# Block-diagonal fp32 products of a decoder trunk cut into 64x64 and 32x32 tiles of the TensorE array

## The reference

```
# A (RWKV-7), 4 heads of 64
kk = kk / max(sqrt(sum(kk*kk over the head)), 1e-12)
mean, var = mean and variance of y over the head;  bonus = sum(r*k*r_k over the head) * v
# B (HGRN2) and C (retention), 4 heads of 64
o * rsqrt(mean(o*o over the head) + EPS)
# C: rotary embedding of q and k, 4 heads of 32 channels each
t1, t2 = split(t, 2);  concat(t1*cos - t2*sin, t1*sin + t2*cos)
# D (RG-LRU), 4 blocks of 64
r = sigmoid(einsum('btgi,gij->btgj', yb, w_a) + b_a);  i = sigmoid(einsum('btgi,gij->btgj', yb, w_x) + b_x)
```

## Time and profile before

| | |
|---|---|
| median of 3 runs | 1134.91 us |
| lowest and highest | 1130.58 and 1135.85 us |
| profiled execution, its own time | 1135.37 us |
| its span (first to last instruction) | 1133.2 us |
| mean granted TensorE clock | 0.976 |
| PE busy | 1086.7 us (96%) |
| DVE, ACT, POOL busy | 586.3, 333.9, 372.9 us |

### The profile page before, as it was taken

One profiled execution on the slowest core, in us unless ns is written; L12 is line 12 of the kernel. 1 busy time (PEld: TensorE's weight loads), 2 busy tenths in 40 slices (PEclk: granted clock), 3 DMA queues, 4 the chain that ended last, 5 costly groups with the idle time before them and its releaser, 6 DMA issues.

```text
span 1133.2 us, 23369 instructions
## 1 busy us (share of the span) xinstructions
PE 1086.7 (96%) x10052; PEld 849.1 (75%) x10052; DVE 586.3 (52%) x1045; ACT 333.9 (29%) x533; POOL 372.9 (33%) x343
## 2 busy tenths in 40 slices
PE   5999999889899999999999999999999989999997
PEld 5876787667677777777777787777777768887885
DVE  3368943885445323333433316747777586423544
ACT  4285212421422222122121133236545341011321
POOL 2231543311316522122212233335433347663000
PEclk8889999989989999999999999999999999999998
DMA  9600111200101011011011021111111116412221
GB/s 356 241 1 19 47 48 55 65 28 24 34 25 38 27 34 39 26 34 39 25 34 35 21 73 37 38 52 40 35 38 35 39 53 249 139 38 93 75 93 56
DMA packets 80134, 70.29 MB, mean 62 GB/s; under 512 B 4128, under 2 KB 68896, under 8 KB 80032
## 3 DMA queue, kind: packets, MB, share of 16 engines
q1 hardware_dynamic: 74560, 49.34, 14.0%
q10 hardware_dynamic: 5472, 19.47, 4.7%
HBM read 64.60 MB, written 4.19 MB: 61 GB/s over the span
## 4 chain that ended last, share of the span: by engine, by line
PE 89%; DVE 7%; ACT 2%; issue 1%; DMA 1%; SPq 0%; ACTq 0%; DVEq 0%
PE bank L581 51%; PE bank L627 8%; PE bank L1082 8%; PE bank L678 4%; PE bank L1043 1%; DVE slots L2060 1%; PE bank L784 1%; DVE slots L1651 1%; PE bank L899 1%; PE bank L903 1%; PE bank L654 1%; PE bank L685 1%; PE bank L815 1%; PE bank L845 1%; PE bank L645 1%
## 5 line engine op out<-in xcount | busy, mean ns | idle before, releaser
L581 PE MATMUL bank<-hn_hi,w_hi 128*128 128x512 f32 x880 | 365.1, 415 | 4.5 <-ACT slots L1194 2.8
L581 PE MATMUL bank<-hn_lo,w_hi 128*128 128x512 f32 x880 | 344.7, 392 | 0.0
L581 PE MATMUL bank<-hn_hi,w_lo 128*128 128x512 f32 x880 | 344.1, 391 | 0.0
L496 POOL CAST w_hi<-w_raw 128x512 fp32r<-128x512 f32 x110 | 86.4, 786 | 573.7 <-PE bank L581 572.4
L581 PEld LDWEIGHTS bank<-hn_hi,w_hi 128*128 128x128 f32 x880 | 165.8, 188 | 46.9 <-issue 4.6
L581 PEld LDWEIGHTS bank<-hn_hi,w_lo 128*128 128x128 f32 x880 | 165.9, 188 | 36.2
L581 PEld LDWEIGHTS bank<-hn_lo,w_hi 128*128 128x128 f32 x880 | 166.3, 189 | 31.4 <-issue 1.9
L498 POOL TENSOR_TENSOR w_lo<-w_raw,w_hi 128x512 fp32r<-128x512 f32 x110 | 155.2, 1411 | 8.8
L1216 ACT ACTIVATE stage<-bank 128x512 f32<-128x512 f32 x64 | 38.3, 598 | 222.7 <-PE bank L581 195.6
L1803 DVE TENSOR_TENSOR stage<-stage,bank 128x512 f32<-128x512 f32 x48 | 33.0, 688 | 64.6 <-PE bank L627 63.5
L1194 ACT ACTIVATE slots<-bank 128x512 f32<-128x512 f32 x42 | 25.1, 598 | 119.7 <-PE bank L581 118.5
(11 more groups left out here) (322 smaller groups left out, 1630.4 us busy)
## 6 DMA issues: line engine op xcount, KB each, us to landing
w_raw<-in_w_in SPq DMA_DIRECT2D x110, 256.0 KB, 2.8
slots<-in_w_mod SPq DMA_DIRECT2D x16, 512.0 KB, 11.2
slots<-in_x SPq DMA_DIRECT2D x8, 512.0 KB, 9.4
w_branch<-in_w_branch SPq DMA_DIRECT2D x32, 128.0 KB, 2.7
slots<-in_w_mod ACTq DMA_DIRECT2D x8, 512.0 KB, 4.8
slots<-in_w_out ACTq DMA_DIRECT2D x8, 512.0 KB, 5.7
xr<-in_x ACTq DMA_DIRECT2D x8, 512.0 KB, 3.6
out<-xr ACTq DMA_DIRECT2D x8, 512.0 KB, 2.6
```

The source lines that it names most:

```text
L496: nc.gpsimd.tensor_copy(w_hi[p][:, :, :], w_raw[p][:, :, :]).then_inc(s_w_hi_ready, 1)
L581: last = mm(o, w[p][:, k4, :], h[:, k, n * HALF:(n + 1) * HALF], start=(p == 0 and k4 == 0 and q == 0), stop=(p == 1 and k4 == 3 and q == 2))
```

## The change

Each of the block-diagonal products is replaced by products of its nonzero blocks, each on its own tile on the diagonal of the array. `over_heads` issues two 64 x 64 products (rows and columns 0 to 63, then 64 to 127), D's gates do the same with `lru_w`, and the rotation issues four 32 x 32 products. All write the same bank as before, each its own partitions, over the same 512 tokens. The semaphore is counted on the last of the two or four. Nothing else is changed, and no product changes its place in the order: 36 products become 80 (8 to 16 gates, 4 to 16 for the rotation, 24 to 48 head sums), which adds 88 matmul records and 88 weight loads.

```
@@ D's gates
-                        mm(bank[q][:, :], lru_w[:, 2 * g + j, :], slot(4 + j)[:, n * HALF:(n + 1) * HALF],
-                           start=True, stop=True).then_inc(s_gates_done, 1)
+                        for r in (slice(0, 64), slice(64, 128)):
+                            last = mm(bank[q][r, :], lru_w[r, 2 * g + j, r], slot(4 + j)[r, n * HALF:(n + 1) * HALF],
+                                      start=True, stop=True)
+                        last.then_inc(s_gates_done, 1)
@@ new, and head_sums
+            def over_heads(o, src):
+
+                for r in (slice(0, 64), slice(64, 128)):
+                    last = mm(o[r, :], blockones[r, r], src[r, :], start=True, stop=True)
+                return last
+
...
-                        mm(bank[4 + 2 * j + n][:, :], blockones,
-                           slot(src + j)[:, n * HALF:(n + 1) * HALF], start=True, stop=True).then_inc(s_head_sums, 1)
+                        over_heads(bank[4 + 2 * j + n], slot(src + j)[:, n * HALF:(n + 1) * HALF]).then_inc(s_head_sums, 1)
@@ the rotation
-                    mm(bank[4 + 2 * q + n][:, :], tb("perm"), slot(20 + q)[:, n * HALF:(n + 1) * HALF],
-                       start=True, stop=True).then_inc(s_rot_done, 1)
+                    for r0 in range(0, P, 32):
+                        r = slice(r0, r0 + 32)
+                        last = mm(bank[4 + 2 * q + n][r, :], tb("perm")[r, r], slot(20 + q)[r, n * HALF:(n + 1) * HALF],
+                                  start=True, stop=True, tile_position=(r0, r0))
+                    last.then_inc(s_rot_done, 1)
@@ A's mean (the bonus at L990 and B's sums at L1069 in the same way)
-                    mm(bank[4 + 2 * j + n][:, :], blockones, slot(4 + j)[:, n * HALF:(n + 1) * HALF],
-                       start=True, stop=True).then_inc(s_a_mean_done, 1)
+                    over_heads(bank[4 + 2 * j + n], slot(4 + j)[:, n * HALF:(n + 1) * HALF]).then_inc(s_a_mean_done, 1)
```

More of the change, by code:

```diff
@@ L989, in _ @@
                     pe.wait_ge(s_roots, 8 + 2 * j + n + 1)
-                    mm(bank[4 + 2 * j + n][:, :], blockones, slot(8 + j)[:, n * HALF:(n + 1) * HALF],
-                       start=True, stop=True).then_inc(s_a_bonus_done, 1)
+                    over_heads(bank[4 + 2 * j + n], slot(8 + j)[:, n * HALF:(n + 1) * HALF]).then_inc(s_a_bonus_done, 1)
             turn_tile(BI)
@@ L1068, in _ @@
                     pe.wait_ge(s_squares, 6 + 2 * n + j + 1)
-                    mm(bank[4 + 2 * j + n][:, :], blockones, slot(12 + j)[:, n * HALF:(n + 1) * HALF],
-                       start=True, stop=True).then_inc(s_head_sums, 1)
+                    over_heads(bank[4 + 2 * j + n], slot(12 + j)[:, n * HALF:(n + 1) * HALF]).then_inc(s_head_sums, 1)
             fill(73)
```

## The result

The changed kernel took **1137.04 us** (median of 20 runs, 1133.69 to 1139.38) against 1134.46 for the kernel before (20 runs, 1130.58 to 1138.03): a ratio of **1.0026**, 95% interval 1.0016 to 1.0037, which is +1.8 to +4.2 us. The forecast was 1136.7 us and +1.8. The profiled execution's span is 1134.9 us, where 1135.0 was forecast.

The account below looks back on a forecast made before the run. TensorE, busy 96% of the span, was taken as the bound. The terms 0 + 0 + 0.15 + 1.48 + 0.15 = 1.78, say +1.8 us, on a median of 1134.91 gave 1136.7 us, range 1131.5 to 1141.5.

Parts of the forecast that it names:

- The streaming term: At every cut product, the blocks run side by side and stream in 0.86 us as before; 0 us added.
- Rival 1: At every burst, tiles writing one bank do not run side by side; head-sum bursts take 6.86 us; 1164 us, chance 0.05.
- rival 4: At the bursts, small tiles are quicker, half the rows or columns halving the record; -10.3 us, 1124.6 us, chance 0.02.
- The switch term: Going between whole-array and tiled products costs TensorE 0.37 us a burst, 0.15 in and 0.22 out; eight bursts.
- The cover: At each burst, switch time ahead of a wait is hidden; D's gates and the rotation were put at 0 us.
- The gates: D's gates: way in hidden by DVE's convolution, way out by PE's wait for ACT; 0 us, bounds -0.05 to 0.37.
- The rotation: DVE takes its first result over 3 us after PE finishes, PE then waits 4.37 us; 0 us, at most 0.37.
- Turn 0: Starts out of a wait, nothing to drain; way out 0.2 less 0.05 for shorter load: 0.15 us, bounds 0 to 0.5.
- Branch B's sums: Way in, 0.15 us, passes down the chain of ACT and DVE; way out vanishes in PE's wait; 0.15 us.
- The waits: PE's waits at L581 for ACT and at L784 and L627 for DVE get shorter by about 0.2 us each.
- Rival 2: The granted clock falls at tiled bursts; one fall 1140.1 us, chance 0.12; two or three 1143 to 1147 us, chance 0.04.
- Rival 3: Nothing is paid at the switches, each being covered or made up by short loads; 1135 us, chance 0.14.

Follow-up runs that it names:

- Alternating the shape: Kernel before with only the head sums tiled, and of these every second product left whole; 1138.27 us, ratio 1.0045.
- the fillings: Kernel before and changed kernel, each with unread fp32r products keeping TensorE busy in four waits; 1130.14 us without tiles, 1130.97 with, before 1134.2.
- gates and rotation alone: Kernel before with only D's gates (64x64) and the rotation (32x32) tiled, head sums whole; 1134.67 us against 1133.35, ratio 1.0017.

## Why the prediction was right

- **The streaming term, 0.** Right. 16 records of 64x64 take 3.65 us and 32 of 32x32 take 3.64, all of one burst into shared banks, where 8 whole ones took 3.60. Rival 1 (1164 us) and rival 4 (1124.6 us) are out by this alone. The rule of the Trainium skill, TensorEngine Tiling (Array Packing), section Gotcha 1: PSUM Pressure, that different row tiles cannot access the same PSUM bank at once, which rival 1 named, does not hold in this form: both blocks wrote one bank for 512 tokens at once, to different partitions. Row tiles that write the same partitions of a bank were not tried.
- **The switch term, 0.37 a burst.** 0.35 at four bursts (turns 1 and 2, the mean, branch B's sums), 0.33 at the rotation, 0.29 at the bonus, behind which transposes follow and not fp32r products. Working it out of L868's burst, on other tiles and 128 tokens, was good enough to 0.02, and the four dense bursts that were put at 1.48 together gave 3 x 0.35 + 0.29 = 1.34, with about 0.04 more close behind each of three of them. Alternating the shape doubled it.
- **The cover.** The gates: way out hidden, and the way in bought 0.05 through the shorter load, in sum -0.07 here and -0.04 to -0.05 in the other traces; I had 0 with a bound of -0.05, and that it is the load was not tried. The rotation: its results were in time, as forecast, but turn 0 came 0.25 later. This is the step that failed, though the forecast of the time came right: I asked whether DVE waits for the products, and not what the 0.33 us of delay does to the casts on GpSimd that TensorE releases, which run beside DVE's steps. It is one of the prediction's own signs of being wrong, a chain on DVE counted as covered that moves PE's next start. The experiment with a whole-array product in place of the tiles gave 0.21 of it; the other 0.04 is not explained.
- **Turn 0, 0.15:** 0.12 between the first traces and 0.06 between the second ones, at a clock that is low for part of the burst; 0.15 with the fillings, at full clock.
- **Branch B's sums, 0.15:** 0.38. The way in cost ACT and DVE 0.155 exactly as put (ACT's first step at 912.32 before and 914.61 after, of which 2.135 had come in earlier). Then a DVE step beside GpSimd's steps took 1.29 where it took 1.07, and 0.21 more went down the chain of reciprocals. By the traces this is the same blind spot as at the rotation; no experiment was made at this place.
- **The waits.** The one at L581 for ACT came out 0.2 shorter, as put, the one ahead of turn 0 only 0.1 shorter, and the one at L627 0.2 longer instead of shorter, since DVE's chain grew by more than TensorE's stream.
- **The sum.** 1.78 forecast, 2.13 in the trace: 0.25 at the rotation and 0.23 at branch B's sums were missing, and 0.13 elsewhere was too much. That the profiled span came within 0.1 us of the forecast is luck: the places outside the change took back 0.44 of the 2.13. The median's +2.6, with +1.8 to +4.2 about it, does not tell these apart, for the places that differ from one execution to the next (branch B's chunks, the low-clock stretches, the first 97 us) move the time by more than the difference.
- **Rival 2, the clock.** It did not fall behind tiled bursts, and it did not for three times as long a burst. Rival 3, nothing paid, falls by the 0.35 in each dense burst.

What stays open: gates and rotation alone measured +0.6 to +3.3 us, and the traced terms explain 0.2 of it. I put the rest to branch B's chunks by one trace, and did not settle whether a kernel's delay shifts their mean, or only chance does, or whether the kernel before ran low in that job.

## What to carry to other kernels

A block-diagonal product does not get quicker by being cut into its blocks: the tiles share the stream of columns, and the zeros between them were free. The cut pays only where the freed tiles get other work at the same time, and it costs a switch of shape, 0.35 us of TensorE's stream for each burst here, so that a few such bursts should stand together or inside stretches that are tiled already. When TensorE is the bound, look at its waits of about 2 us and more before anything else: the work behind them may run at half clock, as it did here in most traces, and products that nobody needs can be cheaper than standing still. A delay that a wait covers on TensorE can still cost something, if it moves another engine's steps against those of the engine that is waited for.

## What the runs showed of the hardware

- Tiles on the diagonal wrote one PSUM bank side by side: 32 records of 512 tokens in 3.64 us, four at a time.
- TensorE started a record for a free tile ahead of three earlier ones that waited for a busy tile: the blocks issued two products apart took 3.70 us, 3.65 in pairs.
- Each change between whole-array and tiled fp32 products cost about 0.17 us, 0.35 for both.
- The granted clock stayed at 1.00 through 10.2 us of four 32x32 tiles. It went to 0.50 behind waits of 1.8 to 4.4 us, though not each time (the wait of 1.80 us ahead of turn 1 had a fall behind it in one trace of twelve), and stayed at 1.00 when they were filled.
- A delay of 0.33 us on TensorE alone lengthened two DVE steps from 0.69 to 0.79 and 0.80 us, at places where GpSimd's casts had moved against them. Two DVE steps that took 1.66 and 1.63 us beside GpSimd's took 0.69 when GpSimd stood still.
